# Decoder trunk on one core: expert-row places that overlap, and three more weight tiles kept in SBUF

## What is computed

```python
u_e = jnp.take(u_tab, eid, axis=0)
act = jax.nn.gelu(jnp.einsum('thkd,td->thk', u_e, xb), approximate=False)
v_e = jnp.take(v_tab, eid, axis=0)
return jnp.einsum('thk,thkd->td', (gate * act).astype(xb.dtype), v_e)
```

## Time and profile before

| | |
|---|---|
| median of 3 runs | 1516.35 us (1516.21 to 1517.46) |
| span of the profiled execution (the profile gives no other time of it) | 1514.4 us |
| busy | PE 1344.1 us (89%), DVE 1050.3 (69%), ACT 633.5 (42%), POOL 608.4 (40%) |
| DMA | 617.17 MB, mean 408 GB/s |
| gathers | 508 whole, 8 of halves; 542.70 MB are on POOL's queue |

### The profile page before, as it was taken

How to read it: one execution, slowest core, us unless ns; L and a number is a source line. 1 busy time by engine, 2 the same in 40 slices (tenths; PEclk the granted TensorE clock), 3 DMA queues, 4 the chain that set the end, 5 groups by cost and what they waited for, 6 DMA issues and landing times.

```text
span 1514.4 us, 15429 instructions
## 1 busy us (share of the span) xinstructions
PE 1344.1 (89%) x4376; PEld 719.9 (48%) x4376; DVE 1050.3 (69%) x2684; ACT 633.5 (42%) x1728; POOL 608.4 (40%) x542
## 2 busy tenths in 40 slices
PE   9999987889787899989988999999999878887776
PEld 7886544445442465444443555445444334442232
DVE  5688677777667768667666666777776766666775
ACT  5665333332233455554433454554343423333333
POOL 0101354444454435334434333434444344544443
PEclk9999999999999899999999999999999999999999
DMA  7897999999999999999999999999999999999997
GB/s 271 290 355 269 424 426 425 427 427 426 426 427 424 424 410 425 426 426 426 427 426 424 424 424 425 424 421 392 426 426 424 427 426 426 427 426 426 426 414 286
DMA packets 96261, 617.17 MB, mean 408 GB/s; under 512 B 10906, under 2 KB 11050, under 8 KB 30640
## 3 DMA queue, kind: packets, MB, share of 16 engines
q0 software_dynamic: 75584, 542.70, 85.6%
q1 hardware_dynamic: 20448, 73.22, 12.5%
q10 hardware_dynamic: 144, 0.26, 0.0%
HBM read 615.09 MB, written 1.05 MB: 407 GB/s over the span
## 4 chain that ended last, share of the span: by engine, by line
PE 24%; DMA 18%; DVE 8%; issue 2%; ACT 1%; POOL 1%; POOLq 0%; ACTq 0%; DVEq 0%
PE psum L1484 24%; DMA row<-in_uv,ids 17%; DVE row L1241 4%; DMA row<-in_uv,half_ids 1%; ACT diag L795 1%; DVE look L1169 0%; DVE numbers L1174 0%; POOL row L575 0%; ACT pick_weight L786 0%; ACT acted L775 0%; DVE look L1172 0%; DVE topi L1108 0%; DVE scores L1100 0%; DVE topi L1097 0%; DVE candpos L1097 0%
## 5 line engine op out<-in xcount | busy, mean ns | idle before, releaser
L1484 PE MATMUL psum<-row,diag 128*128 128x512 f32 x1976 | 931.4, 613 | 154.6 <-ACT diag L795 153.8
L575 POOL DMA_INDIRECT row<-in_uv,ids x508 | 586.3, 1154 | 813.9 <-PE psum L1484 694.7
L1241 DVE SCALAR_TENSOR_TENSOR row<-row,hn 128x1024 f32<-128x1024 f32 x512 | 623.1, 1224 | 375.6 <-DMA row<-in_uv,ids 374.9
L1484 PEld LDWEIGHTS psum<-row,diag 128*128 128x128 f32 x1976 | 367.0, 195 | 625.6 <-issue 374.4
L775 ACT ACTIVATE acted<-dots 128x2 f32<-128x2 f32 x256 | 52.2, 204 | 699.3 <-DVE row L1241 699.1
L795 ACT ACTIVATE diag<-ident,pick_weight 128x128 f32<-128x128 f32 x496 | 175.2, 387 | 2.9 <-PE psum L1484 2.4
L786 ACT ACTIVATE pick_weight<-gate,acted 128x1 f32<-128x1 f32 x496 | 120.3, 287 | 21.9 <-issue 0.4
L942 DVE TENSOR_TENSOR tile_lo<-raw,tile_hi 128x1024 fp32r<-128x1024 f32 x32 | 39.1, 1223 | 27.6 <-ACT tile_hi L621 27.4
L1484 PEld LDWEIGHTS psum<-hT,early_q 128*128 128x128 f32 x256 | 42.3, 204 | 13.8 <-issue 10.9
L1484 PE MATMUL psum<-hT,early_q 128*128 128x128 f32 (+1 forms) x256 | 46.8, 339 | 2.1 <-issue 2.1
L621 ACT ACTIVATE tile_hi<-raw 128x1024 fp32r<-128x1024 f32 x32 | 33.9, 1061 | 34.6 <-PE psum L1484 32.7
(11 more groups left out here) (265 smaller groups left out, 1169.7 us busy)
## 6 DMA issues: line engine op xcount, KB each, us to landing
raw<-in_a_in SPq DMA_DIRECT2D x32, 512.0 KB, 4.8
raw<-in_w_q SPq DMA_DIRECT2D x24, 512.0 KB, 7.9
raw<-in_b_rv SPq DMA_DIRECT2D x19, 512.0 KB, 7.8
row<-in_uv,ids POOLq DMA_INDIRECT x508, 14.8
aout<-in_a_out SPq DMA_DIRECT2D x13, 512.0 KB, 8.2
early_q<-in_w_q SPq DMA_DIRECT2D x12, 512.0 KB, 11.4
raw<-in_b_qk SPq DMA_DIRECT2D x10, 512.0 KB, 8.1
kept<-in_a_out SPq DMA_DIRECT2D x3, 512.0 KB, 14.2
```

The source lines that it names most:

```text
L575: pool.indirect_dma_start(rows[s][:, :], None, t[f"uv{l}"][:, :], bass.IndirectOffsetOnAxis(ids[:, n // TOPK % IDS_GROUPS, k:k + 1], 0)).t ...
L1241: dve.scalar_tensor_tensor(u, u, 1.0, hn[:, h, :], ALU.mult, ALU.mult, accum_out=dots[:, n // TOPK % 2, k:k + 1]).then_inc(dotted, 1)
L1484: return pe.matmul(o, a, b, start=start, stop=stop, skip_group_check=True)
```

## The change

There are 15 places of 4 KB instead of 18. Row n starts at place (13 - 3n) mod 14 and fills it and the next one. Row n+5 starts one place lower, so that its v lies on row n's u. Row n+9 starts one place higher, so its u lies on row n's v. So the gather of row n now waits for two things: the dot of row n-5, and the use of row n-9 as before. The landing semaphores are five instead of nine.

Three of the freed places (15, 16, 17) keep `b_rv` 6, 8 and 14. They are loaded once, early, between the `early_q` loads of places 18 and 20; `b_qk` 1 (`kept[4]`) is moved to the same place in the order.

```diff
-ROW_SLOTS = 9
+ROW_PLACES = 15
+ROW_CYCLE, ROW_STEP, ROW_FIRST = 14, 3, 13
+U_AGE, V_AGE = 5, 9
-AOUT_PLACE = (18, 20, 8, 11, 12, 0, 1, 2, 3, 4, 5, 6, 7)
+AOUT_PLACE = (18, 20, 11, 7, 8, 4, 5, 1, 2, 12, 6, 3, 0)
-SLOT_PLACE = (7, 8, 4, 5, 6, 0, 1, 2, 3)
-SLOT_TILES = (0, 0, 3, 4, 5, 7, 9, 11, 13)
+FIRST_TILES = (0, 3, 5, 7, 9, 10, 10, 11, 12, 13)
-        ("b_rv", 9), ("b_rv", 11), ("b_qk", N_BQK - 1), ("b_rv", 13), ("b_rv", 4)]
+        ("b_rv", 9), ("b_rv", 11), ("b_qk", N_BQK - 1), ("b_rv", 13), ("b_rv", 4), ("b_rv", 6), ("b_rv", 8), ("b_rv", 14)]
+KEPT_BESIDE = {KEPT_RAW + 1: 15, KEPT_RAW + 2: 16, KEPT_RAW + 3: 17}
+def row_place(n):
+
+    return (ROW_FIRST - ROW_STEP * n) % ROW_CYCLE
+                if place == 20:
+                    sp.dma_start(kept[4][:, :], t[KEPT[4][0]][KEPT[4][1]]).then_inc(kept_loaded, 16)
+                    sp.wait_ge(sums_done, 2)
+                    sp.wait_ge(ain_biased, 4 * A_BLOCKS)
+                    for i in KEPT_BESIDE:
+                        sp.dma_start(kept[i][:, :], t[KEPT[i][0]][KEPT[i][1]]).then_inc(kept_loaded, 16)
                 sp.dma_start(early_q[j][:, :], t["w_q0"][RAW_SLOTS + j]).then_inc(early_loaded, 16)
-            sp.dma_start(kept[4][:, :], t[KEPT[4][0]][KEPT[4][1]]).then_inc(kept_loaded, 16)
-                old = n - ROW_SLOTS
-                if 2 <= n < ROW_SLOTS:
-                    pool.wait_ge(other_used, SLOT_TILES[n])
+                old = n - V_AGE
+                if n == 0:
+                    pool.wait_ge(sv_done, 4)
+                elif n < len(FIRST_TILES):
+                    pool.wait_ge(other_used, FIRST_TILES[n])
+                if n >= U_AGE:
+                    pool.wait_ge(dotted, n - U_AGE + 1)
-                s = n % ROW_SLOTS
+                loaded = row_loaded[n % U_AGE]
```

More of the change, by code:

```diff
@@ L282, in trunk @@
         sb("row_gap", [P, 48])
-        places = overlay([(f"row{s}", [P, 2 * D], F32) for s in range(ROW_SLOTS)])
-        rows = [places[s] for s in SLOT_PLACE]
         def wide(place, name, shape, dt=F32):
@@ L292, in from_start, with at_place @@
             return overlay([(name, shape, dt)])[0]
+        def at_place(place, name, shape, dt=F32):
+            return wide(place, name, shape, dt) if place else from_start(name, shape, dt)
+        rows = [at_place(row_place(n), f"row{n}", [P, 2 * D]) for n in range(ROW_CYCLE)]
         yT_hi0, yT_lo0 = wide(9, "yT_hi0", [P, KB, P], F32R), wide(10, "yT_lo0", [P, KB, P], F32R)
@@ L298, in trunk @@
         ln_g, ln_b = wide(26, "ln_g", [P, A_WIDTH]), wide(28, "ln_b", [P, A_WIDTH])
-        aout = [(from_start if place == 0 else lambda *p, place=place: wide(place, *p))(f"aout{c}", [P, TILE]) for c, place in enumerate(AOUT_PLACE)]
+        aout = [at_place(place, f"aout{c}", [P, TILE]) for c, place in enumerate(AOUT_PLACE)]
         tile_hi.append(wide(16, "tile_hi2", [P, TILE], F32R))
@@ L324, in trunk @@
         last_wide = wide(29, "last_wide", [P, TILE])
-        sb("reserved_wide", [P, 30 * TILE])
+        kept_beside = [wide(place, f"kept_beside{place}", [P, TILE]) for place in KEPT_BESIDE.values()]
+        sb("reserved_wide", [P, RESERVED * TILE])
         held = [scores[:, 1, 0:P_HEADS, :].rearrange("p a b -> p (a b)"), last_wide, scores[:, 1, P_HEADS:P_ROWS, :].rearrange("p a b -> p (a b)")]
@@ L329, in trunk @@
         aout += kept[:N_AOUT - len(AOUT_PLACE)]
-        kept += [*kept_wide, kept_gain, raw[RING]]
+        kept += [*kept_wide, kept_gain, raw[RING], *kept_beside]
         w_g2 = qT[0:G_ROWS, :, P:T]
@@ L389, in trunk @@
         scores_copied = [sem(f"scores_copied{l}") for l in range(2)]
-        row_loaded = [sem(f"row_loaded{s}") for s in range(ROW_SLOTS)]
+        row_loaded = [sem(f"row_loaded{s}") for s in range(U_AGE)]
         dotted, gelu_done, diag_ready, row_used = sem("dotted"), sem("gelu_done"), sem("diag_ready"), sem("row_used")
@@ L1237, in dot @@
                 _, h, g, k = group_of(n)
-                s = n % ROW_SLOTS
-                dve.wait_ge(row_loaded[s], row_turn(n))
-                u = rows[s][:, 0:D]
+                dve.wait_ge(row_loaded[n % U_AGE], row_turn(n))
+                u = rows[n % ROW_CYCLE][:, 0:D]
                 dve.scalar_tensor_tensor(u, u, 1.0, hn[:, h, :], ALU.mult, ALU.mult, accum_out=dots[:, n // TOPK % 2, k:k + 1]).then_inc(dotted, 1)
@@ L1259, in last_sums @@
                     after(summed)
-                    ins = dve.scalar_tensor_tensor(first, rows[(2 * ROWS - LAST + i) % ROW_SLOTS][:, D:D + BANK], last_weight[:, i:i + 1], first,
+                    ins = dve.scalar_tensor_tensor(first, rows[(2 * ROWS - LAST + i) % ROW_CYCLE][:, D:D + BANK], last_weight[:, i:i + 1], first,
                                                    ALU.mult, ALU.add)
@@ L1831, in _ @@
                         last = w == PICKS - 1 or n == 2 * ROWS - LAST - 1 and d == 0
-                        ins = product(psum[:, 4 + 2 * h + d, :], diag[:, m % DIAGS, :], rows[n % ROW_SLOTS][:, D + d * BANK:D + (d + 1) * BANK],
+                        ins = product(psum[:, 4 + 2 * h + d, :], diag[:, m % DIAGS, :], rows[n % ROW_CYCLE][:, D + d * BANK:D + (d + 1) * BANK],
                                       start=w == 0, stop=last)
```

15 lines of the change are left out of this document (8 added, 7 removed).

## The result

The changed kernel takes 1521.35 us (median of 6 runs, 1518.61 to 1525.14), the kernel before beside it 1516.6 us (6 runs, 1515.61 to 1517.46). The ratio of the times, changed kernel over kernel before, is 1.0033, with a 95% interval of 1.0023 to 1.0043: slower by 5.0 us, where 2 us less were forecast. A repeat later (`e18_change_again`) gave 1.0027 (1.0017 to 1.0038). The profiled execution of the change was a long one of 1524.84 us, span 1523.0; so its times are read as places and shapes, and costs are taken from the ratios. Rows (gathers, dots) are counted from 0 in the order in which they run.

A forecast was written before the change was run, and what follows sets the result against it. DMA was taken as first bound, TensorE second, in the mixers. Terms +0.8 - 3.7 + 0.9 - 3.7 + 3.7 + 0.3 - 0.2 + 0.2 - 0.3 = -2.0 us from 1516.35 gave 1514.3 us, range 1509.6 to 1520.

The forecast's parts named there:

- The loads removed: In the GLA mixers, three tiles fewer per half save 3.7 us of DMA time each, 7.4 us together.
- The start: From about 137 us, three tiles loaded once beside the first gathers cost +0.8 us, bounds 0 and 1.2.
- case C: Rival: early tile loads delay the start while TensorE is full, losing 3.7 us, giving 1518.0 us; chance 0.06.
- the queue behind row 0 covers: At the start, first rows gathered later for other aout tiles; the queue was to cover that, so no cost was added.
- The wait for a dot: On POOL, gathers wait for the dot five rows back; cost 0.3 + 0.2 = 0.5 us, at rows 318 and 360.
- +0.7 us to spare at row 190: Behind the first gated r, the gather five rows on had 0.7 us before the slowest DMA engine runs dry.
- If it never runs dry: The most loaded of sixteen DMA engines sets the time from 145 us to the end; the others may idle.
- Case B: Rival: the shallower queue runs dry behind late dots, with landings of 8.2 us, giving 1525.8 us; chance 0.14.
- Half 0's and half 1's savings: In the mixers, half 0 leaves DMA 2.0 us ahead; half 1's 3.7 us turn into idle DMA before row 323's gather.
- Case A: Rival: TensorE doesn't hold DMA back in the mixers, both halves count, -6.6 us, giving 1509.8 us; chance 0.20.
- The signs named: Signs of being right: 13 b_rv loads, landings near 11 and 5.6 us, dot waits, DMA holes near 1019 and 664.
- the rest moved 2 us ahead: Sign of being right: after the start, with its first product unmoved, everything else comes 2 us earlier.

The follow-up runs named there:

- e18_change_again: The change as it is, measured again beside the same runs of the kernel before: ratio 1.0027.
- e11_tiles_wait5: Kernel before without the six b_rv 6, 8, 14 loads (products read kept tiles), each gather also waiting for the dot five rows back: ratio 1.0015.
- e3_silu_after: Changed kernel with the gated r (SILU) moved two rows later on VectorE, from w = 61 to w = 63: ratio 0.9989 to the kernel before.
- e16_tiles5_silu: Kernel before without the six b_rv loads, with the wait for the dot five rows back and SILU moved from 61 to 63: ratio 0.9970.
- e8_no_start: Changed kernel with SILU at 63 and without the three early kept-tile loads, products reading tiles already kept: ratio 0.9986 to the kernel before.
- e1_wait5: Kernel before with one more wait, each gather from row 5 on waiting for the dot five rows back: ratio 1.0035, 5.3 us slower.
- e12_tiles_wait6: Kernel before without the six b_rv loads (products read kept tiles), each gather also waiting for the dot six rows back: ratio 0.9965.
- e2_tiles: Kernel before without the six loads of b_rv 6, 8 and 14, products reading kept tiles, no added wait: ratio 0.9959, 6.2 us faster.

## Why the prediction was wrong

*The loads removed, -7.4 us.* Nearly right: 6.2 us measured alone.

*The start, +0.8.* Too small, though not for the loads that it priced: half a microsecond was measured for these three. In the profile the three tiles land between 137 and 145 us, as forecast, and TensorE is never idle there, so case C did not come. But the change is 1.8 to 2.7 us slower than `e11_tiles_wait5` (two runs of the one, 1.0027 and 1.0033, against 1.0015), and `e3_silu_after` 2.9 us slower than `e16_tiles5_silu`. Between these pairs lie the new places, the first rows' waits for other aout tiles, and the start. The loads explain half a microsecond of it. Dot 100 comes 2.5 to 4.9 us later than in the kernel before in all five profiles with this layout, also in that of `e8_no_start` (2.5), which has no such loads. In the four with the wait for five rows and the layout of before it comes 0.2 to 3.9 us later, so single executions don't part the wait from the layout. That "the queue behind row 0 covers" the later first gathers was argued, and was not measured by itself; it stays open.

*The wait for a dot, +0.5: the step that failed.* It costs 5.3 us (`e1_wait5`, interval 3.2 to 7.3). Its building blocks were nearly sound. Issue to landing with nothing queued was taken as 5.6 us; gather 195 at 669.00 was there for dot 195 at 674.80, 5.8 us, and gather 323 took 6.4. Some luck was in that: of the 0.9 us added for a gather's issue the rows give only 0.6. The Trainium skill, "DMA: Bandwidth & Descriptors", section "Latency and other measured facts", gives HBM access 2 us at high load, from which the prediction made an estimate of 7.4 us. These two gathers do not show that time, and they do not test the figure either, since the load was low: 0 GB/s in 670 to 671 and in 1023 to 1025 us. What failed is what was made of them: +0.7 us to spare at row 190, -0.3 at row 318, -0.2 at row 360, and so a cost of 0.3 + 0.2. The sum counted the lateness of one gather as the whole cost of a place, and looked at four places. The rows show three things that it left out. (1) A hole isn't over when it ends: the next rows come 3.4 to 3.9 us apart, not 2.46 (674.80, 678.65, 682.05; 1029.25, 1032.62). (2) "If it never runs dry", of the slowest of the sixteen engines, "the others may idle" took that engine's time as the measure. In the changed kernel all sixteen stood, for the 2 us from 1023 to 1025 (share 0.00, 0 GB/s):

```profile
1023.00:1025.00 2.00, 0.09 (x1) 0.09 (x1) 2.00 (x5) 1.12 (x5) 1.70 (x2) 0.68 0.00 0
```

(3) The forecast's spare times were read at the moments of the kernel before, and the changed kernel doesn't keep these moments: dot 190 came at 667.15 (666.75 in `e18_change_again`) and not 1.3 us earlier than 664.79. That these three add up to 5.3 us is argued, not measured. Case B had this mechanism, at the right places, though by the wrong number (landings of 8.2 us) and with dips behind all choices, where the dip at row 365 is the one clearly seen.

*Half 0's and half 1's savings.* The step that half 1's 3.7 us turn into idle DMA was right: DMA stands until gather 323 of 1022.89 brings it new work, and `e12_tiles_wait6` and `e16_tiles5_silu` keep the gain by one more row or by a dot that isn't late. The 2.0 us kept of half 0's were too kind: the same hole, at gather 195, takes all of it back (dot 189 +1.3, dot 200 +4.2 us). Forecast was a gain of 2.0 + 0. With the old layout the runs give 6.2 less about 3; with the change's about nothing, since 5.0 measured less 5.3 for the wait and 0.5 for the loads at the start leave -0.8. Case A fell for this kernel. With nine rows it came near: `e2_tiles` gained 6.2 us of 7.4, so TensorE holds the gain back only where the queue is shallow.

*The signs named.* 13 `b_rv` loads, landings near 11 and 5.6, waits named after dots, a hole near 1019 and one near 664: all came, though the second hole lasted until about 1025, and the first was not small (226 GB/s in 665 to 670 us). Each of them follows from the structure of the change, and none of them tested the price. The sign that did was "the rest moved 2 us ahead"; dot 318 came 3.7 us later instead (1021.39, 1017.69).

What stays open is how `e1_wait5`'s 5.3 us are shared out. Its profiled execution was its quickest (1518.09 us beside a median of 1521.42), and shows only 1.5 us of them. Open too is what makes the changed kernel late in its first 100 rows. And why SILU at 63 does nothing for the wait alone, but gives 6.8 us once the loads are gone, is told by the waits only in part.

## What to carry to other kernels

Measure a queue's depth by where its filler waits at the worst moment, not by its median. Five rows of 2.46 us looked like 12.3 us against 7.2 needed, and a stall of 9.7 us on another engine emptied the queue; with six rows a stall as long cost nothing measurable (`e12_tiles_wait6` beside `e2_tiles`). When two ages share a memory (five and nine here), move the cut between them before giving up: 16 places with six and nine, and two tiles kept instead of three, gave 0.9983 where the change beside it has 1.0027, with nothing moved on VectorE.

A saving of transfers and a shallower queue need not be independent terms. Here the saving moved the consumer up against the next engine's late point, where the shallow queue could not bank it; the size of this, about 3 us, is uncertain, but the 6.8 us that came back with the late point moved are not. Price the two together, or take the interaction as a term of its own.

## What the runs showed of the hardware

Behind a gap, in which its queue ran dry or nearly so, DMA was slower for some microseconds at about the same busy share. Stretches of `e1_wait5`, behind the late dot of row 360 and in steady flow:

```profile
1135.00:1140.00 5.00, 5.00 (x25) 3.30 (x24) 2.86 (x6) 1.43 (x6) 2.94 (x3) 1.00 0.97 329
...
1350.00:1480.00 130.00, 99.20 (x214) 38.80 (x212) 87.54 (x235) 41.42 (x139) 51.79 (x53) 0.99 1.01 425
```

At a busy share of 0.97 the engines moved 329 GB/s; in steady flow 425 at 1.01. The changed kernel shows it from 1025 to 1030 us: 338 GB/s at 0.93. Per busy time that is 14 to 19% less. At 338 GB/s a row of 1.049 MB takes 3.1 us, which goes far to explain why the rows behind the gap come 3.4 us apart. No run shows why the engines are slower there. I had taken a restarted queue to run at full rate at once.
